# A fused transformer stack on one Trainium2 core: seven-product gate and up pairs in both gated feed-forwards, activation sums one set per output block up to the fourth

## The reference

```python
def swiglu(x, w_gate, w_up, w_down):
    return (jax.nn.silu(x @ w_gate) * (x @ w_up)) @ w_down

h = h + 0.5 * swiglu(rmsnorm(h, ffn1_norm), ffn1_w_gate, ffn1_w_up, ffn1_w_down)
h = h + mixer(rmsnorm(h, mix_norm))                 # ends in w_out, stage wout1
h = h + 0.5 * swiglu(rmsnorm(h, ffn2_norm), ffn2_w_gate, ffn2_w_up, ffn2_w_down)
gate = jax.nn.sigmoid(rmsnorm(h, ple_gate_norm) @ ple_w_gate)
h = h + gate * rmsnorm(p @ ple_w_proj, ple_norm)
```

## Time and profile before

| | us |
|---|---|
| median of three runs | 2253.64 |
| the profiled execution | 2255.11 |
| its span | 2253.3 |
| TensorE busy (matmuls) | 2224.9 |
| VectorE busy | 1337.6 |
| ScalarE busy | 892.6 |
| GpSimd busy | 321.0 |

### The profile page before, as it was taken

One profiled execution on the slowest core, in us unless ns is written; L12 is line 12 of the kernel. 1 busy time (PEld: TensorE's weight loads), 2 busy tenths in 40 slices (PEclk: granted clock), 3 DMA queues, 4 the chain that ended last, 5 costly groups with the idle time before them and its releaser, 6 DMA issues.

```text
span 2253.3 us, 30491 instructions
## 1 busy us (share of the span) xinstructions
PE 2224.9 (99%) x12660; PEld 1855.0 (82%) x12667; DVE 1337.6 (59%) x1562; ACT 892.6 (40%) x1190; POOL 321.0 (14%) x191
## 2 busy tenths in 40 slices
PE   9999999999999999999999999999999999999999
PEld 7888888878888888888886789899876858898998
DVE  6434446597644345475557675576567874855754
ACT  4222234345422332353238543344434574533532
POOL 2000001030100100021002123123100301231230
PEclk9999999999999999999999999999999999999999
DMA  5233322320233323232320133333333201334332
GB/s 190 94 94 94 111 75 86 101 72 20 84 99 107 93 94 93 76 111 94 113 75 20 55 107 111 122 112 104 99 115 80 72 20 45 115 112 122 106 110 94
DMA packets 201186, 208.12 MB, mean 92 GB/s; under 512 B 7042, under 2 KB 195218, under 8 KB 201076
## 3 DMA queue, kind: packets, MB, share of 16 engines
q1 hardware_dynamic: 201076, 206.56, 29.6%
HBM read 199.27 MB, written 2.10 MB: 89 GB/s over the span
## 4 chain that ended last, share of the span: by engine, by line
PE 91%; DVE 6%; ACT 2%; issue 1%; DMA 0%; SPq 0%; ACTq 0%; DVEq 0%
PE psum L867 78%; PE psum L957 4%; PE psum L955 4%; PE psum L956 4%; DVE sm L2880 1%; DVE w_lo L404 1%; DVE rstd L2287 0%; PE psum L1409 0%; PE psum L1401 0%; DVE free_x L2269 0%; ACT w_hi L391 0%; ACT free_h L1685 0%; DVE free_h L2272 0%; DVE free_x L3002 0%; DVE sm L3000 0%
## 5 line engine op out<-in xcount | busy, mean ns | idle before, releaser
L867 PE MATMUL psum<-xg_lo,w_hi 128*128 128x512 f32 (+1 forms) x1576 | 608.5, 389 | 0.4 <-ACT free_x L1685 0.4
L867 PE MATMUL psum<-xg_hi,w_hi 128*128 128x512 f32 (+1 forms) x1528 | 596.2, 390 | 3.9 <-DVE xg_lo L2269 1.7
L867 PE MATMUL psum<-xg_hi,w_lo 128*128 128x512 f32 (+1 forms) x1528 | 592.9, 388 | 0.0
L391 ACT ACTIVATE w_hi<-w_raw 128x2048 fp32r<-128x2048 f32 (+1 forms) x148 | 281.6, 1903 | 382.9 <-PE psum L867 363.3
L404 DVE TENSOR_TENSOR w_lo<-w_raw,w_hi 128x2048 fp32r<-128x2048 f32 (+1 forms) x146 | 340.9, 2335 | 151.2 <-ACT w_hi L391 148.0
L867 PEld LDWEIGHTS psum<-xg_lo,w_hi 128*128 128x128 f32 x1576 | 295.6, 188 | 62.2 <-ACT free_x L1685 1.4
L867 PEld LDWEIGHTS psum<-xg_hi,w_hi 128*128 128x128 f32 x1528 | 287.0, 188 | 68.0 <-issue 4.9
L867 PEld LDWEIGHTS psum<-xg_hi,w_lo 128*128 128x128 f32 x1528 | 286.9, 188 | 59.5
L867 PE MATMUL psum<-h_hi,w_hi 128*128 128x512 f32 x696 | 278.1, 400 | 3.1 <-DVE w_lo L404 2.8
L867 PE MATMUL psum<-h_hi,w_lo 128*128 128x512 f32 x696 | 271.8, 391 | 0.0
L867 PE MATMUL psum<-h_lo,w_hi 128*128 128x512 f32 x696 | 271.8, 390 | 0.0
(11 more groups left out here) (347 smaller groups left out, 3468.8 us busy)
## 6 DMA issues: line engine op xcount, KB each, us to landing
w_raw<-in_mlp_w SPq DMA_DIRECT2D x36, 1024.0 KB, 5.2
w_raw<-in_ffn_w_gate SPq DMA_DIRECT2D x21, 1024.0 KB, 5.3
w_raw<-in_ffn_w_up SPq DMA_DIRECT2D x21, 1024.0 KB, 5.3
w_raw<-in_mlp_w SPq DMA_DIRECT2D x42, 512.0 KB, 4.9
w_raw<-in_ffn_w_down SPq DMA_DIRECT2D x16, 1024.0 KB, 5.1
w_raw<-in_diff_w_in SPq DMA_DIRECT2D x12, 1024.0 KB, 5.1
w_raw<-in_w_in SPq DMA_DIRECT2D x9, 1024.0 KB, 5.2
w_raw<-in_dsa_w_in SPq DMA_DIRECT2D x9, 1024.0 KB, 5.2
```

What stands on the lines that cost most here:

```text
L391: e.activation(w_hi[:, wside(c), 0:n], w_raw[:, c % 2, 0:n], ACT.Copy).then_inc(sem("hi_done"), 1)
L867: return pe.matmul(out, lhsT, rhs, start=start, stop=stop)
```

## The change

Both gated feed-forwards join `FAST`. ffn1 keeps two plain pairs in its first group and ffn2 one (`PLAIN`); the other 9 and 10 pairs are seven-product pairs of one gate and one up block, unrolled. New functions `fast_gated` on ScalarE and VectorE replace the loops there. ffn1's activation sums are made during its second plain pair through one buffer, `trig`; ffn2's behind wout1's second, third and fourth block, and in wout2 the sets 0, 1 and 2 move from blocks two, two and three to blocks two, three and four. The scratch area grows from 10752 to 14336 columns, constants and the embedding move to its new end, the embedding's input p is loaded in ffn2 and not in wout1, its sum and rms use the sine tables' buffers. GpSimd runs the row additions of all four feed-forwards; in ffn2's second group the embedding's eight-tile sum stands between the first addition and the others, and the load of `w_third` waits for it.

```diff
--- before.py
+++ after.py
     return np.ascontiguousarray(g.T)
 
 
-FAST = ("mlp0", "mlp1")
+FAST = ('ffn1', 'ffn2', 'mlp0', 'mlp1')
+PLAIN = {"ffn1": 2, "ffn2": 1, "mlp0": 1, "mlp1": 1}
+STAGE = {"ffn1": 0, "ffn2": 2, "mlp0": 5, "mlp1": 7}
 
 
...
+        X_WITH = {"wout1": ((), (0,), (1,), (2,)), "wout2": ((), (0,), (1,), (2,)), "wout3": ((0,), (1,), (2,), ())}
+
+        def x_raw(p, i):
+
+            return trig if p == 0 else (buf_a, buf_c)[i % 2]
...
                     if q == 0:
-                        sp.wait_ge(sem("ssq_done"), 7 * (p + 1))
+                        sp.wait_ge(*(third_free or (sem("ssq_done"), 7 * (p + 1))))
                     else:
...
+                    if wg is not None and name in FAST:
+                        vg, vu = (rows(w, 0, KT)[:, :, P * f0:P * (f0 + tiles)] for w in (wg, wu))
+                        ahead = PLAIN[name] if g == 0 else 0
+                        for j in range(skip, ahead):
+                            load(sp, c + 2 * j, 0, vg[:, :, j * BC:(j + 1) * BC])
+                            load(sp, c + 2 * j + 1, 0, vu[:, :, j * BC:(j + 1) * BC])
+                        fast_loads(group_first[name, g], p, lambda q: (vu[:, :, (q + ahead) * BC:(q + ahead + 1) * BC],
+                                                                       vg[:, :, (q + ahead) * BC:(q + ahead + 1) * BC]),
+                                   (sem("emb_ssq"), 7) if (name, g) == ("ffn2", 1) else None)
...
-                        fast_up(c + 2 if g == 0 else c, p)
+                        for j in range(1, PLAIN[name] if g == 0 else 0):
+                            blk(c + 2 * j, a=xg(p))
+                            blk(c + 2 * j + 1, a=xg(p))
+                        fast_up(group_first[name, g], p)
...
+                def silu(q):
+                    if q >= 0:
+                        act.wait_ge(sem("gate_scaled"), made[q] + 1)
+                        a(buf_a[:], buf_a[:], ACT.Silu).then_inc(sem("silu"), 1)
...
+                    t = 2 * (q + ahead)
+                    act.wait_ge(sem("hmul"), h0 + q + 1)
+                    a(hidden(p)[0][:, t:t + 2, :], buf_b[:], ACT.Copy).then_inc(sem("h_hi_done"), 1)
+
+                for q in range(len(made)):
+                    split(7 * q + 3)
+                    silu(q - 1)
+                    copy(q, 0)
+                    split(7 * q + 4)
+                    hidden_hi(q - 1)
+                    copy(q, 1)
+                    split(7 * q + 5)
+                    copy(q, 2)
+                    for n in range(6, 10):
+                        split(7 * q + n)
+                q = len(made) - 1
+                hi(act, after)
+                silu(q)
+                hidden_hi(q)
+                hi(act, after + 1)
...
+                        for j in range(last):
+                            gated_pair(j, first=True)
+                        if ahead:
+                            if p == 0:
+                                for i in range(2):
+                                    x_scale(p, i)
+                                    x_high(p, i)
+                                hi(act, c0)
+                            act.wait_ge(sem("evac"), c0 - 1)
+                            a(buf_c[:], buf_a[:], ACT.Silu).then_inc(sem("silu"), 1)
+                            if p == 0:
+                                for i in range(2, 4):
+                                    x_scale(p, i)
+                                    x_high(p, i)
+                            for n in range(2, 4):
+                                strip_hi(act, c0, n)
+                        fast_gated(c0, p, h0 + ahead, s0 + ahead, ahead, plain_hi)
...
+                def last_quarter(q):
+                    if q >= 0:
+                        dve.wait_ge(*strip_mark("pe", c0, 7 * q + 6))
+                        tt(buf_b[:, :, TS:S], by_halves(pair_banks(c0, q)[0]), scale[:, :, TS:S], ALU.mult).then_inc(sem("evac"), 1)
+
+                def gate_up(q):
+                    if q >= 0:
+                        dve.wait_ge(sem("evac"), c0 + 2 * q + 2)
+                        dve.wait_ge(sem("silu"), s0 + q + 1)
+                        tt(buf_b[:], buf_b[:], buf_a[:], ALU.mult).then_inc(sem("hmul"), 1)
...
+                for q, pair in enumerate(made):
+                    run, side_sum, first_sum = pair_banks(c0, q)
+                    last_quarter(q - 1)
+                    split(7 * q + 3)
+                    gate_up(q - 1)
+                    split(7 * q + 4)
+                    hidden_lo(q - 1)
+                    split(7 * q + 5)
+                    split(7 * q + 6)
+                    dve.wait_ge(*strip_mark("pe", c0, 7 * q + 3))
+                    dve.wait_ge(sem("h_done"), h0 + q)
+                    tt(buf_b[:, :, 0:TS], by_halves(first_sum), scale[:, :, 0:TS], ALU.mult)
+                    split(7 * q + 7)
+                    dve.wait_ge(*strip_mark("pe", c0, 7 * q + 4))
+                    tt(buf_a[:, :, TS:S], by_halves(run), by_halves(buf_c[:, q % 2, :]), ALU.add).then_inc(sem("u_read"), 1)
+                    split(7 * q + 8)
+                    if q == len(made) - 1:
+                        if len(made) % 2:
+                            lo_half(dve, after, 0, odd_turn[c0])
+                        else:
+                            lo(dve, after)
+                    dve.wait_ge(*strip_mark("pe", c0, 7 * q + 5))
+                    tt(buf_a[:, :, 0:TS], by_halves(side_sum), by_halves(buf_d[:, q % 2, :]), ALU.add).then_inc(sem("evac"), 1)
+                    if q == len(made) - 1 and len(made) % 2:
+                        lo_half(dve, after, 1, odd_turn[c0])
+                    dve.wait_ge(sem("u_read"), pair + 1)
+                    dve.wait_ge(sem("evac"), c0 + 2 * q + 1)
+                    stt(buf_a[:], buf_a[:], -1.0, scale, ALU.mult, ALU.mult).then_inc(sem("gate_scaled"), 1)
+                    split(7 * q + 9)
+                q = len(made) - 1
+                last_quarter(q)
+                gate_up(q)
+                hidden_lo(q)
                 lo(dve, after + 1)
 
             def residual(c, i, scale, p_next):
...
+                        for j in range(last):
+                            gated_pair(j, first=True)
+                        if ahead:
+                            if p == 0:
+                                for i in range(2):
+                                    x_split(p, i)
+                                    x_low(p, i)
+                            evac_scaled(c0 - 2, buf_a)
+                            if p == 0:
+                                lo(dve, c0)
+                                for i in range(2, 4):
+                                    x_split(p, i)
+                                    x_low(p, i)
+                            evac_scaled(c0 - 1, buf_b)
+                            dve.wait_ge(sem("evac"), c0)
+                            dve.wait_ge(sem("silu"), s0 + ahead)
+                            tt(buf_d[:], buf_b[:], buf_c[:], ALU.mult).then_inc(sem("hmul"), 1)
+                            for n in range(2, 4):
+                                strip_lo(dve, c0, n)
+                        fast_gated(c0, p, h0 + ahead, s0 + ahead, ahead, plain_lo)
...
+            def other_sums(c0):
+
+                made = fast_groups[c0]
+                for q, pair in enumerate(made):
+                    c = c0 + 2 * q
+                    pool.wait_ge(sem("w22_in"), 16 * (pair + 1))
+                    pool.wait_ge(*strip_mark("lo", c0, 7 * q + 1))
+                    add_rows(w_run[run_half[pair]], raw22(c0, q), sem("w_next"))
+                    pool.wait_ge(sem("w21_third_in"), 16 * (pair + 1))
+                    add_rows(w_third, raw22(c0, q), sem("w_third"))
+                    if q + 1 < len(made):
+                        first_sum(c0, q + 1)
+                    pool.wait_ge(sem(f"landed{(c + 1) % 2}"), 16 * ((c + 1) // 2 + 1))
+                    pool.wait_ge(*strip_mark("lo", c0, 7 * q + 2))
+                    add_rows(w_run[run_half[pair]], raw(c + 1, 0), sem("w_next"))
+
+            def fast_sums(name, with_first=None):
+
+                for g in range(len(GROUPS[name]) if name in FAST else 0):
+                    c0 = group_first[name, g]
+                    first_sum(c0, 0)
+                    if with_first and g == 1:
+                        with_first()
+                    other_sums(c0)
```

More of the change, by code:

```diff
@@ L275, in program @@
             for g, tiles in enumerate(GROUPS[name]):
-                first, n_pairs = at[name, g, "up"] + (2 if g == 0 else 0), tiles // per - (g == 0)
+                plain_pairs = PLAIN[name] if g == 0 else 0
+                first, n_pairs = at[name, g, "up"] + 2 * plain_pairs, tiles // per - plain_pairs
+                group_first[name, g] = first
+                if n_pairs % 2:
+                    odd_turn[first] = len(odd_turn)
+                if per == 2:
+                    gated_pairs += n_pairs
```

(31 more changed lines are left out.)

155 lines of the change are left out of this document (91 added, 64 removed).

## The result

The changed kernel takes 2278.18 us, the median of four runs (2276.93 to 2279.28), beside 2255.05 for the kernel before on the same chip (2253.39 to 2257.74): ratio 1.0102, 95% interval [1.0088, 1.0116]. It is slower, by 23 us where 13.6 were forecast, and 4 us outside the range of 2256 to 2274. The profiled execution has a span of 2275.9 us, 22.6 more than before.

A forecast was written before the change was run, and what follows sets the result against it. The prediction took TensorE, busy 99% of the span, as the bound. Costs of 48.7 us against gains of 35.1 made it 13.6 us slower than the 2253.6 median: 2267, range 2256 to 2274.

The forecast's parts named there:

- The gain per pair: Both feed-forwards: a seven-product pair takes 19.94 us against 21.77 plain, 1.83 less; 19 pairs take 34.8 us off TensorE.
- (e): Inside groups, from the second pair on: GpSimd additions delay VectorE, so TensorE waits for ScalarE's third copy; 21.0 us in all.
- (c): Entry of ffn2: activation sums between residual stretches make strip 2 late; 2.5 us, 0 without collisions.
- rival 1: Inside groups: entries cost as forecast, but the waits there don't come; 2246 us, chance 0.20.
- E: Start of the pair in mlp0 used as measure, 1398.5; TensorE's fifth product is due 11.4 us after it.
- (a): Entry of ffn1: product 1 waits for four activation sums, slowed by GpSimd additions; 9 us, bounds 3 and 11.2.
- (b): Third group of ffn1: first copy stands behind ScalarE's last Sin, so product 2 waits; 5.1 us, bounds 4 and 6.
- (d): Second group of ffn2: embedding's squares on GpSimd and loads behind them delay the first copy; 6.0 us, bounds 5 and 7.
- (f): Down block after the third groups: hidden tiles and second weight block come 0.3 us late, twice; 0.6 us.
- wout2: Moved activation set removes a 2.77 us wait and its clock loss, but the wait returns at mlp0's strip 3; 0.3 gain.
- (g): TensorE's clock after waits: 1.5 us each at (a), (b) and (d), 4.5 in all; none counted inside groups.
- Rival 4: Inside groups: the waits there cost clock too; 2275 us, chance 0.10.

## Why the prediction was right or wrong

Step by step, forecast against the trace, in us:

- The gain per pair, 1.83: right, but 0.2 us is lost at each wait (3.2 in all, an estimate), which I had not counted.
- (e) 21.0 against 15.5 (the 15.8 of the waits on `buf_d`, less the 0.30 that belongs to (c)). The mechanism was right in every row, and rival 1, its absence, did not come. The first middle wait of a group was forecast at 2.4 and measured 2.05 to 2.40; but the lag did not grow (2.85 forecast, 2.08 and 2.23 measured), and two last pairs waited 0.29 and 0.16, the other four 0.13 or less, and not 0.25 and 0.6. By its own terms the forecast's last pair ends at E + 11.5 and not at E + 11.7. Why the lag is not carried on, no run shows.
- (a) 9 against 9.8; (c) 2.5 against 2.4; (b) 5.1 against 4.7; (d) 6.0 against 4.7. (f) 0.6 against nothing. Some of these hits are luck. The terms named in (a) add up to 22.3 and not 20.0, and its lower bound of 3 measured 1.9 + 0.6 without the additions. (b) is 6.25 when the clock holds ahead of it, beyond its bound of 6. The 1.56 at 906.29 was not seen: VectorE's angles meet the additions there, and the wait goes with either of them.
- wout2, 0.3 against 0.0 in its own run, which can't tell them apart. Between ffn2's end and its own the changed trace is 2.6 shorter than the one before (25.2 late at the one, 22.6 at the other). 1.6 of that has nothing to do with wout2: it is one stretch of the attention ahead of it, here in windows of the kernel before and after:

```profile
1173.67:1181.45 7.78, 7.25 (x38) 4.29 (x38) 4.97 (x13) 4.80 (x17) 1.45 (x2) 0.78 0.01 2
```

```profile
1198.79:1204.96 6.17, 5.71 (x39) 3.47 (x39) 4.98 (x13) 4.80 (x17) 1.46 (x2) 1.00 0.00 0
```

The same work took 7.78 us at a mean clock of 0.78 and 6.17 at 1.00. A clock loss that the first execution happened to have is missing in the second. About 1.0 is left for wout2 and mlp0's entry.
- **(g), the step that failed.** "The waits inside groups are near or below that length; I count none there, at most 5 x 1.5 = 7.5." There were seven such waits and not five (two in each of the groups of four pairs, one in each of the three groups of three, and (e)'s own sum has seven), and five of them cost 1.7 each, 8.4. At (a), (b) and (d) I allowed 4.5; it was 2.6 + 2.6 + 2.5 = 7.7. Forecast 4.5, measured 16.1 behind waits, and 1.7 more that no wait explains: an error of 13.3 in a total error of 9. It was not larger only because others went the other way, (e) by 5.5 and (d) by 1.3 above all. Rival 4 had this mechanism and, at 2275, nearly the time; I gave it 0.10, because the one row at hand, the wait of 2.77 us, was longer. A bound from a single row said nothing about waits 0.7 us shorter, and should have been taken as open on both sides.

The sum closes: waits 38.7 in the two feed-forwards, clock 17.8, restarts 3.2, less 34.8 is 24.9; the marks at ffn2's end stand 25.2 apart (985.6 and 1010.8).

## What to carry to other kernels

Price a new wait on TensorE at its length, plus 0.2 for the restart, plus a loss of clock from about 2 us on: here 1.7 us behind five of seven waits of 2.05 to 2.40, and 2.5 or 2.6 behind those of 4.7 and 9.8. A wait of 2 us is then nearly twice what the list of waits shows. Take a wait and the clock ahead of it together: where another engine sets the wait's end, what TensorE gains before it comes back as wait. Before moving work from a full engine to idle ones, ask whether those engines exclude each other: here VectorE was busy for 89% and GpSimd for 42% of the pairs that mattered, where the whole span had 69% and 24%. A scheme that works once behind a long entry can lose its gain at every entry, so put the entry's own preparation first and give one unit of the gain for it.

## What the hardware did that I had not expected

Waits of 2.05 us were followed by 1.2 GHz in some pairs and not in others of the same code; one of 2.40 kept 2.4 GHz, one of 3.22 in another run did not. None of the waits of 1.73 us or less before a product did, but in the attention of the kernel before a stretch behind a wait of 1.02 us had a mean clock of 0.78, and at ffn1's `setup` it fell in half of the profiled executions with no wait at all. Behind the middle waits the low clock lasted 3.4 us, behind the wait of 9.82 us 5.3.

VectorE's operations with one on-chip operand are held up too. Its timeline at the beginning of ffn1's third group, while no addition runs, and of ffn2's, while they do:

```profile
288.13 0.43 DVE L2383 TENSOR_SCALAR buf_a<-buf_a 128x512 f32<-128x512 f32 x1
288.59 0.43 DVE L2382 TENSOR_SCALAR buf_a<-buf_a 128x512 f32<-128x512 f32 x1
...
892.51 2.12 DVE L2383 TENSOR_SCALAR buf_a<-buf_a 128x512 f32<-128x512 f32 x1
894.67 2.50 DVE L2382 TENSOR_SCALAR buf_a<-buf_a 128x512 f32<-128x512 f32 x1
```

0.43 us against 2.12 and 2.50. The Trainium skill names this case as well (SBUF — State Buffer, section "Who interferes with whom"): a `tensor_scalar` may enter a mode that uses both port pairs, and then it contends with GpSimd like an operation of two inputs. The rows agree.
